# A head's root taken before the next head's values, its keys transposed first into another bank, and the state stores awaited at the program's end

## The reference, cut to what matters

```
proj = h @ w_in                            # q, k, v, o of a head: 256 columns each
num = w_inter * (q @ C) + (q k^T * decay) @ v       # for each direction
h = num / max(|den|, exp(-m))
hm = (hf + hb) * sigmoid(o)
hm = hm * rsqrt(mean(hm*hm) + EPS) * head_norm      # over the head's 256 channels
C_new = decay * C + (wk * k)^T @ v                   # of the 128 context tokens, an output
```

## Time and profile before

| | us |
|---|---|
| median of 3 runs | 1840.29 |
| lowest and highest | 1839.6, 1842.44 |
| the profiled execution | 1844.41 |
| its span | 1842.6 |
| TensorE busy | 1692.6 (92%) |
| VectorE busy | 574.4 (31%) |
| ScalarE busy | 374.8 (20%) |

### The profile page before, as it was taken

The page is one execution under the profiler, slowest core; times in us unless marked ns, Lnnn a source line. Parts: engine busy times, 40 slices in busy tenths (PEclk is TensorE's granted clock), DMA queues, the critical chain, the costliest instruction groups (busy, mean ns, idle before and its releaser), DMA issues. The chain is left out here.

```text
span 1842.6 us, 33652 instructions
## 1 busy us (share of the span) xinstructions
PE 1692.6 (92%) x15258; PEld 962.0 (52%) x15258; DVE 574.4 (31%) x1314; ACT 374.8 (20%) x777; POOL 101.8 (6%) x95
## 2 busy tenths in 40 slices
PE   5889999999899898979995799999999999999993
PEld 2456666546455464669883344444444444444441
DVE  5569991013013131357647001111111111111113
ACT  3343332121211313145434100000000000000001
POOL 0810000000000000000000000000000000000000
PEclk9889999999899898989998899999999999999997
DMA  9335455101202021043315889999999999999963
GB/s 382 113 93 177 156 188 228 46 0 32 83 1 103 12 80 46 18 165 139 121 62 205 318 349 384 404 403 404 399 401 405 400 410 405 405 406 401 404 252 129
DMA packets 56916, 420.61 MB, mean 228 GB/s; under 512 B 10932, under 2 KB 17588, under 8 KB 26948
## 3 DMA queue, kind: packets, MB, share of 16 engines
q1 hardware_dynamic: 49188, 386.97, 52.9%
q0 software_dynamic: 6864, 28.85, 5.2%
q10 hardware_dynamic: 720, 2.62, 0.4%
HBM read 391.86 MB, written 24.42 MB: 226 GB/s over the span
## 5 line engine op out<-in xcount | busy, mean ns | idle before, releaser
L1742 PE MATMUL bank<-place,x 128*32 128x384 f32 x3120 | 258.1, 489 | 0.9 <-ACT x L1805 0.9
L1742 PE MATMUL bank<-ring_tail,x 128*32 128x384 f32 x3024 | 249.7, 488 | 1.4 <-issue 1.4
L1742 PEld LDWEIGHTS bank<-place,x 128*32 128x32 f32 x3120 | 100.4, 110 | 147.4 <-issue 143.9
L1742 PEld LDWEIGHTS bank<-ring_tail,x 128*32 128x32 f32 x3024 | 98.2, 110 | 145.0 <-issue 143.7
L1836 DVE SCALAR_TENSOR_TENSOR hT<-bank,gvr,xT 32x256 f32<-32x256 f32 (+1 forms) x192 | 92.2, 480 | 240.9 <-PE bank L1772 238.3
L1850 DVE TENSOR_TENSOR xT<-sq,bank 128x384 f32<-128x384 f32 x48 | 23.7, 549 | 443.6 <-issue 362.6
L1065 PE MATMUL bank<-place,hT 128*128 128x512 f32 x320 | 138.0, 592 | 0.0
L242 PE MATMUL bank<-hT,xT 128*128 128x512 f32 x256 | 133.6, 604 | 1.1 <-ACT qk L252 0.9
L1772 PE MATMUL bank<-place,xT 128*32 128x256 f32 x2304 | 128.0, 379 | 0.0
L1772 PE MATMUL bank<-ring_tail,xT 128*32 128x256 f32 x2304 | 127.8, 379 | 0.0
L1442 PE MATMUL bank<-a_h,w_h 128*128 128x320 f32 x320 | 101.0, 316 | 19.5 <-DVE w_l L1514 16.9
(11 more groups left out here) (364 smaller groups left out, 1913.3 us busy)
## 6 DMA issues: line engine op xcount, KB each, us to landing
place<-w_e_dram SPq DMA_DIRECT2D x97, 1536.0 KB, 11.4
ring_tail<-w_e_dram SPq DMA_DIRECT2D x95, 1536.0 KB, 11.6
place<-w_ada_dram SPq DMA_DIRECT2D x12, 2048.0 KB, 9.2
xT<-w_gate_dram POOLq DMA_DIRECT2D x8, 1024.0 KB, 6.5
place<-w_qk_dram SPq DMA_DIRECT2D x4, 2048.0 KB, 11.5
place<-w_vo_dram SPq DMA_DIRECT2D x4, 2048.0 KB, 11.6
place<-w_pAB_dram SPq DMA_DIRECT2D x4, 1536.0 KB, 7.8
hT<-gates_dram SPq DMA_DIRECT2D x4, 1280.0 KB, 5.9
```

Source lines behind the costliest of these rows:

```text
L1742: mm = pe.matmul(PS[bank + j][TJ * g:TJ * g + TJ, 0:FC], x[:, e % 2, 2 * c + k, TJ * j:TJ * j + TJ], w[:, k, FC * g:FC * g + FC], start=(c ...
```

## The change

Three edits, all at the boundary between two heads.

ScalarE's root gets a function of its own, `root(h)`, called between `inter(h)` and the next head's `out_vo` (for the last head, ahead of gate unit 15's sigmoids). The keys' transposes come first in `turn(h)`, ahead of the wait for `hn_ready`, into bank 2, with a signal of their own, `k_turned`; for the last head they wait for the sigmoids of gate unit 15, which read that bank. VectorE waits for `k_turned` in place of `ha_ready` and reads bank 2. And the wait for the stores of states moves from GpSimd at the end of the block to SyncE at the end of the program.

```diff
@@ gpsimd, mLSTM block @@
-                pool.wait_ge(sem("c_out"), 32 * H)
@@ tensor, turn(h) @@
                     b = h % 2
+                    if h + 1 == H:
+                        pe.wait_ge(sem("gate_sig"), NU)
+                    for k in range(2):
+                        mm = pe.transpose(PS[2][:, k * P:(k + 1) * P], qk[:, b, 2 + k, LAT:TOK], ident)
+                    mm.then_inc(sem("k_turned"), 1)
                     pe.wait_ge(sem("hn_ready"), h + 1)
...
-                        if r == 2:
-                            for k in range(2):
-                                o = (2 + k) * P
-                                mm = pe.transpose(PS[bank][:, o:o + P], qk[:, b, 2 + k, LAT:TOK], ident)
                         mm.then_inc(sem("h_turned"), 1)
@@ scalar @@
-                def finish(h):
+                def root(h):
                     act.wait_ge(sem("ms_inv"), h + 1)
                     act.activation(rs5[:], ssq[:], ACT.Sqrt).then_inc(sem("rs_ready"), 1)
+
+                def finish(h):
...
                     inter(h)
+                    root(h)
                     if h + 1 < H:
                         out_vo(h + 1)
@@ vector, finish(h) @@
-                    dve.wait_ge(sem("ha_ready"), 3 * h + 3)
+                    dve.wait_ge(sem("k_turned"), h + 1)
                     for d in range(2):
-                        ins = dve.tensor_scalar(kw[:, d, :], PS[4][:, 2 * P:4 * P], wk[:, d:d + 1], None, ALU.mult)
+                        ins = dve.tensor_scalar(kw[:, d, :], PS[2][:, 0:2 * P], wk[:, d:d + 1], None, ALU.mult)
@@ sync, last block @@
                 sp.wait_ge(sem("out_done"), 16 * NT)
+                sp.wait_ge(sem("c_out"), 32 * H)
```

## The result

The changed kernel takes 1816.28 us (median of 4 runs, 1814.69 to 1817.62) against 1840.19 us; the ratio is 0.9859, 95% interval 0.9842 to 0.9876. Measured again, beside the kernel before, it gave 1814.33 against 1840.51 us, ratio 0.9851 (0.9839 to 0.9864). The prediction was 1807.5 us, with a range of 1802 to 1816. The profiled executions differ by 29.1 us (1844.41 to 1815.35); that of before lay above nearly all its runs, so the trace shows some 3 to 5 us more than the medians.

A forecast was written before the change was run, and what follows sets the result against it. TensorE, busy for 92% of the span, was taken as the bound, with gains in its idle or slow stretches. Savings of 17.5 + 5.0 + 4.4 + 5.9 = 32.8 us off 1840.3 gave 1807.5 us, range 1802 to 1816.

The forecast's parts named there:

- three signs of being wrong: Wrong if stretch stays above 8 us, scores' clock 0.85 or below, or next block 4 us or more after stores' issue.
- The place and the mechanism: Between heads: root, load and scaling leave the path, TensorE's 3.71 us idle goes; keys are weighed during h's transposes.
- The new stretch: From projection's end to next head's scores: 6.05 us in place of 12.42, 11.83 and 11.42, together 17.5 us saved.
- The last head: Behind gate unit 15: stretch of 6.9 us instead of 11.90, 5.0 us saved, extra table loads hidden.
- The block's end: With no store awaited, next block begins at 794.5 instead of 798.98: 4.4 us saved.
- third rival: Block's end still waits for the stores, GpSimd being held by what it issued: 1811.9 us, chance 0.11.
- The clock: Scores of heads 1 to 3 run like head 0's, 10.36 us at clock 1.00: 5.9 us saved, bound 0.
- second rival: Clock falls all the same: 1813.4 us, or 1816 to 1817 if it falls inside the stretch; chance 0.17.

The follow-up runs named there:

- `wait_only`: Kernel before with only the wait for the stores moved to the program's end: 1842.58 us, ratio 1.0010.
- `spread_wide`: Changed kernel with the maxima spread from 128 partitions (124 of them zeros) in place of 4, by the same four products: 1809.3 us, ratio 0.9815.
- `store_sp`: Changed kernel with the last head's state stores issued by SyncE in place of GpSimd: 1813.91 us, ratio 0.9859.
- `store_sp_fill`: Changed kernel, last head's stores issued by SyncE, five unread 128x512 products in each hole of the projections: 1814.82 us, ratio 0.9849.
- `best2`: Changed kernel, SyncE last stores, third and fourth state products in banks 0 and 1, 128-row spread, shorter unread products in projection holes: 1802.67 us, ratio 0.9793.

## Why the prediction was right, and where its terms were off

The result lies 0.3 us beyond the upper end of the range, the second measurement (1814.33) inside it; the direction and the order of the gain were right (23.9 to 26.2 us by the medians, 29.1 by the trace, against 32.8). But two of the prediction's own three signs of being wrong came: the clock in the scores stayed at 0.85 or below, and the next block starts over 4 us behind the stores' issue. That the time came out near is partly luck: two terms were too small by 5.2 us together (stretches and last head), two too large by 8.8 us (block's end and clock). By its steps:

- *The place and the mechanism* were right: root, load and scaling off the path, keys weighed under the transposes. Both waits went, each by its own edit.
- *The new stretch*: 6.05 forecast, 4.71 measured, so 21.5 us saved in place of 17.5. All three parts of the sum were too long: to the first eviction of h 1.26 forecast and 0.69 measured, from there to the first copy of a state 2.33 and 1.94, from there to the scores 2.46 and 2.08. The mis-sized terms were durations of slow stretches, taken for durations at full clock. The 2.06 us of ten transposes ran mostly at half clock; with the clock at 1.00 ten take 1.25 us. The six evictions of h took 2.33 us beside them and take 2.08 now, and the 2.46 us of the earlier trace rows stand at a granted clock of 0.71. The first eviction of h now starts when ScalarE is through with the projection (489.59), which the sum did not have in it at all. The windows of the kernel before show the slow clock, had they been asked of this group:

```profile
603.56:604.00 0.44, 0.44 (x4) 0.44 (x5) 0.00 (x0) 0.00 (x0) 0.00 (x0) 0.96 0.00 0
604.00:606.04 2.04, 2.04 (x11) 1.64 (x8) 0.00 (x0) 1.65 (x4) 0.00 (x0) 0.50 0.00 0
```

- *The last head*: 5.0 forecast, 6.2 measured, by the same misreading. The two table loads more are there and hidden; the one ahead of the second normalisation's root runs at 936.71, and ScalarE still waits 5.37 us behind it.
- *The block's end* failed: 4.4 forecast, 0.5 measured (1.4 in the trace of `wait_only`, nothing in its times). The third rival, at 0.11, named what happens: GpSimd is held there by what it has issued. The row that I took for a free block end had no fresh store of GpSimd behind it, and I had said so and weighed it too lightly.
- *The clock* failed: 5.9 forecast, 1.0 measured for heads 1 to 3, and head 0 lost 1.1. The step that failed is the inference from the earlier trace rows, "no wait ahead of head 0, so 1.00": I laid the low clock in the scores to the holes ahead of them, when head 0 was merely spared in that execution (in the ten traces with these four products made once it is at 1.00 in four and at 0.85 in six). `spread_wide` shows the cause: products over 4 rows. The rule of the Trainium skill (TensorE: Matmul & The Clock Gate, section on psum-queue depth-cycling) on short idles between groups of matmuls that cycle through banks, which stood beside the second rival, came to the right side, but these waits do not by themselves lower the clock in this case: with the same waits of 0.78 and 0.47 us and wide products it is 1.00 throughout.

The second and the third rival held together, which no rival of mine had; with my own stretch they give 1807.5 + 5.9 + 4.4 = 1817.8 us. Stretches that were shorter than I had summed brought the time down from that.

Open is why the low stretches in the projections hit some executions and not others: that they are the clock behind the holes is shown (`store_sp`, holes open, 0.93; `store_sp_fill` and `best2`, filled, 1.00), what decides in which execution they come is not, for the same holes stand in the changed kernel at 1.00. No run of `store_sp` was as fast as one without the loss should be, but four runs cannot settle that. Nor is it shown whether GpSimd waits at a block's end for the landing itself (3.8 us behind an issue here) or for something near it.

## What to carry to other kernels

An operation that heads a serial chain and whose input is ready long before belongs at the first place where its engine is idle; two waits in one chain can be taken out separately, and here their gains added. Before a duration is carried over from a trace, ask for the granted clock of that very stretch, for a row behind an idle hole can be a row at half clock. A semaphore wait that is taken away frees little if the engine that issued the DMAs is held at the block's end anyway: let another engine issue the last ones, and then look at the next stage, which may give the time back.

## What the runs showed of the hardware that was not expected

Products over 4 rows lower TensorE's clock though TensorE is never idle: with the four spreading products (4x512 and 4x128) the scores take 11.4 to 14.1 us in 32 of 40 cases, made twice 15.3 to 17.0 us, and over 128 rows, zeros but for four, 10.3 to 10.4 us in 12 of 12. A block's end behind two fresh stores of GpSimd comes 4.8 to 5.7 us after the first one's issue though nothing waits for them, behind the same two stores issued by SyncE 1.33 us after. And the same three holes of 2.6 us in TensorE's work bring the clock down in some traces (0.93 over a group) and not in others (1.00), which is worth 4 to 5 us.
